# A mixture of experts' gate and up projections: the up projection's weights in 128-column loads instead of 64-column ones

## The reference

```python
def expert_choice_ffn(h, router_w, w1, w3, w2):
    n = B * T
    cap = max(1, EC_CAPACITY_FACTOR * n // N_EXPERTS)
    xf = h.reshape(n, D)
    aff = jax.nn.softmax(jnp.dot(xf, router_w).astype(jnp.float32), axis=-1)
    gate, idx = lax.top_k(aff.T, cap)
    xe = xf[idx]
    hid = jax.nn.silu(jnp.einsum('ecd,edf->ecf', xe, w1)) * jnp.einsum('ecd,edf->ecf', xe, w3)
    ye = jnp.einsum('ecf,efd->ecd', hid, w2) * gate[..., None].astype(h.dtype)
    out = jnp.zeros_like(xf).at[idx.reshape(-1)].add(ye.reshape(-1, D).astype(xf.dtype))
```

## Time and profile before

| | us |
|---|---|
| median of three runs | 1811.71 |
| lowest and highest of them | 1809.51, 1817.16 |
| the profiled execution, its own time | 1815.41 |
| its span, first to last instruction | 1813.6 |

### The profile page before, as it was taken

One profiled execution on the slowest core, in us unless ns is written; L12 is line 12 of the kernel. 1 busy time (PEld: TensorE's weight loads), 2 busy tenths in 40 slices (PEclk: granted clock), 3 DMA queues, 4 the chain that ended last, 5 costly groups with the idle time before them and its releaser, 6 DMA issues.

```text
span 1813.6 us, 40314 instructions
## 1 busy us (share of the span) xinstructions
PE 1588.8 (88%) x17797; PEld 1051.5 (58%) x17797; DVE 680.9 (38%) x1411; ACT 437.5 (24%) x742; POOL 253.6 (14%) x263
## 2 busy tenths in 40 slices
PE   5999989999798789899999999888889959877976
PEld 2554436645366567666655477566665546665755
DVE  4534676722711111113149465554461342111112
ACT  3145315510311111113011254523220320000100
POOL 0000000000111111000000044355430011112111
PEclk9999999999899999898999999999899979888988
DMA  9534434052899999934211100011117159999981
GB/s 349 183 134 159 155 118 99 1 232 100 333 307 358 369 343 353 339 74 156 91 49 50 47 1 1 2 49 65 58 40 319 54 192 354 328 334 359 335 283 23
DMA packets 89967, 326.27 MB, mean 180 GB/s; under 512 B 11556, under 2 KB 17304, under 8 KB 81592
## 3 DMA queue, kind: packets, MB, share of 16 engines
q1 hardware_dynamic: 75824, 284.80, 42.8%
q0 software_dynamic: 9648, 32.65, 6.7%
q10 hardware_dynamic: 4312, 6.03, 0.9%
HBM read 301.30 MB, written 22.16 MB: 178 GB/s over the span
## 4 chain that ended last, share of the span: by engine, by line
PE 69%; DVE 7%; issue 7%; ACT 1%; DMA 1%; POOL 0%; POOLq 0%; ACTq 0%; DVEq 0%
PE pairs L225 18%; PE pairs L1611 17%; PE pairs L1623 6%; PE pairs L1628 3%; PE pairs L1594 2%; PE pairs L1251 2%; PE pairs L358 1%; PE pairs L2154 1%; PE pairs L2134 1%; PE pairs L1265 1%; PE pairs L2360 1%; PE pairs L2117 1%; PE pairs L2371 1%; PE pairs L749 1%; DVE arena L1535 1%
## 5 line engine op out<-in xcount | busy, mean ns | idle before, releaser
L225 PE MATMUL pairs<-hT,ring 128*128 128x128 f32 (+1 forms) x1120 | 306.0, 435 | 2.2 <-ACT hT L372 2.2
L1611 PE MATMUL pairs<-arena 128*64 128x80 f32 x5632 | 228.5, 247 | 77.0 <-issue 76.0
L1611 PEld LDWEIGHTS pairs<-arena 128*64 128x64 f32 x5632 | 221.5, 149 | 89.7 <-issue 89.6
L225 PEld LDWEIGHTS pairs<-hT,ring 128*128 128x128 f32 x1120 | 170.3, 192 | 138.5 <-issue 138.4
L372 ACT ACTIVATE arena<-pairs 128x512 f32<-128x512 f32 (+6 forms) x214 | 124.6, 598 | 390.4 <-PE pairs L225 126.4
L225 PE MATMUL pairs<-ring,hT 128*128 128x512 f32 (+1 forms) x448 | 178.4, 557 | 0.0
L1685 DVE TENSOR_TENSOR arena<-arena,pairs 128x160 f32<-128x160 f32 x64 | 20.6, 321 | 350.1 <-PE pairs L1611 350.1
L225 PEld LDWEIGHTS pairs<-ring,hT 128*128 128x128 f32 x448 | 84.4, 190 | 90.1 <-issue 87.1
L1611 PE MATMUL pairs<-arena,ring 128*64 128x80 f32 x2560 | 93.2, 233 | 8.3 <-issue 8.2
L1611 PEld LDWEIGHTS pairs<-arena,ring 128*64 128x64 f32 x2560 | 90.4, 137 | 13.8 <-issue 13.8
L1623 PE MATMUL pairs<-arena 128*64 128x512 f32 x352 | 83.1, 599 | 0.5 <-issue 0.3
(11 more groups left out here) (402 smaller groups left out, 2253.3 us busy)
## 6 DMA issues: line engine op xcount, KB each, us to landing
arena<-in_exp_w SPq DMA_DIRECT2D x66, 2048.0 KB, 12.0
ring<-in_exp_w SPq DMA_DIRECT2D x30, 2048.0 KB, 16.5
ring<-in_w_mod SPq DMA_DIRECT2D x24, 2048.0 KB, 8.3
ring<-in_w_in_ab SPq DMA_DIRECT2D x5, 2048.0 KB, 13.2
ring<-in_w_in_cd SPq DMA_DIRECT2D x5, 2048.0 KB, 8.4
ring<-in_w_out SPq DMA_DIRECT2D x4, 2048.0 KB, 11.0
h_rows<-arena POOLq DMA_DIRECT2D x10, 512.0 KB, 3.5
arena<-moe_rows ACTq DMA_DIRECT2D x4, 640.0 KB, 6.6
```

Source lines behind the costliest of these rows:

```text
L225: last = pe.matmul(out, lhs(k), rhs(k), start=(k == 0), stop=(k == KD - 1))
L1611: last = pe.matmul(lin_of(j, f)[c:c + 64, :], w[:, k, f * P + c:f * P + c + 64], rhs, start=(k == 0), stop=(k == KD - 1))
```

## The change

In the loop over `k`, the width of a block is now 64 for j = 0, as before, and 128 for j = 1. So for W3 a block of 128 features is one matmul with 128 stationary columns that writes all 128 partitions, in place of two with 64 columns. The matmul calls for W3 fall from 64 to 32 for an expert. What is computed, the order of the sums over `k`, the semaphores and everything on the other engines stay.

```diff
                         for k in range(KD):
                             rhs = xeT[:, k // 4, CAP * (k % 4):CAP * (k % 4) + CAP]
-                            for c in range(0, P, 64):
-                                last = pe.matmul(lin_of(j, f)[c:c + 64, :], w[:, k, f * P + c:f * P + c + 64], rhs,
+                            n = (P if j else 64)
+                            for c in range(0, P, n):
+                                last = pe.matmul(lin_of(j, f)[c:c + n, :], w[:, k, f * P + c:f * P + c + n], rhs,
                                                  start=(k == 0), stop=(k == KD - 1))
```

## The result

| | us |
|---|---|
| before, median of 4 runs | 1810.61 |
| changed, median of 4 runs (1784.42 to 1790.96) | 1787.16 |
| ratio, changed to before | 0.9866, 95% interval 0.9834 to 0.9898 |
| span of the changed kernel's profiled execution | 1789.1 |

The change makes the kernel faster by 1.3% (by the interval, 1.0 to 1.7%). The forecast was 1868, slower by 3%.

What follows compares the result with a forecast made beforehand. The prediction took TensorE, waiting for blocks of its own instructions, to bound the expert stages. Slower matmuls, +83 us, less 27 given back made +56 on 1811.7, so 1868 us, range 1840 to 1900.

Steps and rivals of the forecast that it cites:

- Which engine sets the pace, and with what: Expert stages: TensorE sets the pace, waiting for blocks of its own instructions, not weights; stops total 84.1 us.
- The matmuls, +83 us: W3 product: 64 wide records at 110 ns replace 128 narrow at 34.7, +2.60 us an expert, +83 over 32.
- What is given back, 27 us: Expert turns: fewer records and slower work per instruction block remove nearly all stops inside the turns, giving back 27 us.
- The jumps stay, 41.8 us: Turn ends: eight jumps back still refetch the head's block, at 4.9 to 5.7 us each, 41.8 together.
- the stops behind the head stay also: Behind each turn's short head block: eight stops, 19.6 us together, stay because the W1 records there are untouched.
- the inner stops: Inside the turns, at instruction blocks eaten faster than they come: 22.7 us of stops, nearly all expected to go.
- The first: W3 product: the wide load hides behind the matmul at 69.3 ns a record, nothing added; 1785 us, chance 0.09.
- The second: Expert stages: less dense DMA halves jumps, head stops and low clock, -43 us beside -27; 1825 us, chance 0.06.
- The third: Wide W3 products: TensorE's clock falls to 1.2 GHz in a third of them, 75 us more; 1943 us, chance 0.05.
- The signs named: Trace signs: W3's wide records in 7.0 us, experts 18.1, turns 63 and 66, seven or eight packets, "<-issue" 62 us.

Runs made afterwards that it cites:

- the written-out pair: TensorE's sixteen experts of each stage written out without a loop: the kernel before so edited, 1739.70 us, and the changed kernel so edited, 1788.42 us.

## Why the prediction was wrong

- *Which engine sets the pace, and with what.* Right: TensorE, held up by blocks of its own instructions. Weight transfers were late in no kernel at 49 us a turn or more.
- *The matmuls, +83 us.* Right: 2.66 us an expert, +85; 110 ns a record was forecast, 114 and 113 measured. It is the pace of the rows that load 128 columns for one or for 128 moving ones.
- *What is given back, 27 us.* This is the step that failed: "The jumps stay, 41.8 us: a turn still ends in one, and the head's block is fetched as before", and "the stops behind the head stay also". They went, all of them, and with them the low clock behind (0.96 and 0.92 in the turns before, 1.00 now): 85.1 + 23.5 = 109 us were given back, not 27. Of the 82 us more, 61.4 are the stops that were kept; the rest, some 20, is by subtraction the low clock and the refills behind them. For the inner stops the sum was about right, as the written-out pair shows: 49 us slower with the change, 56 forecast.
- *Where the reasoning slipped.* The prediction counted the fetches of a turn (nine packets) and the body's blocks, but took it as given that a body is fetched anew in every turn. It never asked how long a body may be for that not to be so, though the edit cut just this length by a fifth. That a body over seven blocks stays and one over eight doesn't could not be read from the trace of before, as TensorE has no other loop there. A threshold should have been a rival, with a chance of its own. The Trainium skill (Runtime: NRT & Kernel Launch, section Instruction fetch mechanics) gives TensorE a buffer of 128 KiB, 2048 instructions, and says that a taken branch stalls if its target isn't in the current window of two pages; the prediction cited the stall and neither the size nor the condition. The runs agree that there is a condition, but not with two pages, and they stay one block below the eight of the size: 1773 instructions in seven blocks jump back without a stop, 1645 in eight don't.
- *The rivals.* The first gave 1785 and a time within 3 us of the measured one, by a mechanism that is wrong: the load doesn't hide, a wide record is 114 ns and not 69. The second (fetching relaxes since the weights come less densely) is wrong as well: the DMA engines are fuller than before, 1.02 of a share against 0.95 to 0.99. The third, a falling clock, did not occur: 1.00 in the turns shown.
- *The signs named.* Wide records and an expert of 18.1 us came as said; turns of 63 and 66 us, seven or eight packets in them and 62 us of "<-issue" did not: a turn took 54.6 us, with no packet and no such stop.

Open: why seven and not eight blocks. That one place goes to the block next in order would fit the packets, one more in a turn than the blocks touched, but was not tried by itself; nor was the smallest stretch by which an eighth block spoils it.

## What to carry to other kernels

When a trace shows "<-issue" stops at fixed records of a hardware loop, count the body's instructions and the blocks of 256 they touch, and compare with what stays: here seven. Around that border a few instructions more or less, or instructions far ahead of the loop that only shift it, were worth 76 and 109 us, about as much as the 85 us of work that the edit adds. So price an edit of a loop body by its work and by its length separately, and if a dearer form is used to shorten the body, use it only as often as needed: one product in three, not in every expert, gave 5.0% in place of 1.3%, but only with the borders shifted; without the shift it gave 0.7%.

## What was not expected of the hardware

- A loop of 1517 to 1773 instructions over seven blocks runs on TensorE without fetching; over eight blocks nine come in each turn, over nine ten, so also those that would have fitted.
- A jump back over eight or nine blocks costs 2.7 to 2.9 us with the DMA engines 38% busy and 4.9 to 5.8 us at 92 to 100%.
- A stretch of wide loads with 80 moving columns kept a granted clock of 1.00 (2.4 GHz) where it had it, but in the kernel with all products wide, where layer 0's first expert began at 0.50 (1.2 GHz), it stayed there for 27.4 us. In the changed kernel the same expert starts with narrow products, and its clock was 0.58 in the first 5 us and 1.00 in the next 9, as the rows below show. It is one stretch of each kind; that the form of the loads made the difference was not tested.

```profile
506.00:511.00 5.00, 5.00 (x86) 5.00 (x88) 0.00 (x0) 0.00 (x0) 0.13 (x1) 0.58 0.67 159
511.00:520.00 9.00, 9.00 (x115) 8.91 (x112) 0.36 (x2) 1.72 (x2) 0.00 (x0) 1.00 0.61 235
```
